# Two-layer transformer block with expert routing: five of six modulation products move from TensorE to folded row sums on VectorE, and three expert loads wait for stored rows

## The reference, cut to what matters

```
silu_c = jax.nn.silu(c)
silu_cc = jax.nn.silu(c_ctx)
for l in range(DEPTH):                       # DEPTH = 2
    mod = silu_c @ w_ada[l] + b_ada[l]
    sh1, sc1, gt1, sh2, sc2, gt2 = [m[:, None, :] for m in jnp.split(mod, 6, axis=-1)]
    modc = silu_cc @ w_ada[l] + b_ada[l]
    shc1, scc1, gtc1, shc2, scc2, gtc2 = jnp.split(modc, 6)
    h = modulate(rmsnorm(x, g_mix[l]), sh1, sc1)
    p = h @ w_in[l]
    x = x + gt1 * latent_mixer(p, ...)       # attention, windowed attention, short conv; gates; w_out
    h2 = modulate(rmsnorm(x, g_ffn[l]), sh2, sc2)
    x = x + gt2 * expert_choice_ffn(h2, ...) # router, top-k tokens of each of 16 experts, 3 matmuls
    # in layer 0 the same for the ctx tokens, with shc1 ... gtc2
```

## Time and profile before

| what | value |
|---|---|
| median of 3 runs | 3529.16 us (3526.13 to 3535.64) |
| the profiled execution's own time | 3529.06 us |
| its span | 3527.3 us |
| TensorE busy | 3276.5 us, 93% of the span |
| VectorE busy | 1242.0 us, 35% |
| ScalarE busy | 1004.1 us, 28% |
| mean granted TensorE clock | 0.979 of 2.4 GHz |
| DMA | 617.00 MB |

### The profile page before, as it was taken

How to read it: one execution, slowest core, us unless ns; L and a number is a source line. 1 busy time by engine, 2 the same in 40 slices (tenths; PEclk the granted TensorE clock), 3 DMA queues, 4 the chain that set the end, 5 groups by cost and what they waited for, 6 DMA issues and landing times.

```text
span 3527.3 us, 48003 instructions
## 1 busy us (share of the span) xinstructions
PE 3276.5 (93%) x21246; PEld 2201.5 (62%) x21250; DVE 1242.0 (35%) x1821; ACT 1004.1 (28%) x1571; POOL 221.3 (6%) x142
## 2 busy tenths in 40 slices
PE   6999999999699999989999996988879999989998
PEld 4787667888334343467768882332327766858887
DVE  3335642233401011145563333111126444353333
ACT  3623541122210001037343222000022354342223
POOL 0100000121000000001000220000002010020000
PEclk9999999999799999999999998999999999999999
DMA  7540014221899999743102329999983121323331
GB/s 216 149 144 25 1 49 120 66 61 60 323 399 398 390 351 395 299 65 83 39 1 72 96 90 370 421 421 421 421 321 86 34 59 37 96 60 96 101 96 66
DMA packets 385614, 617.00 MB, mean 175 GB/s; under 512 B 99234, under 2 KB 288896, under 8 KB 360704
## 3 DMA queue, kind: packets, MB, share of 16 engines
q1 hardware_dynamic: 378064, 596.50, 47.9%
q0 software_dynamic: 4384, 15.73, 1.3%
q10 hardware_dynamic: 2960, 1.71, 0.2%
HBM read 606.54 MB, written 7.34 MB: 174 GB/s over the span
## 4 chain that ended last, share of the span: by engine, by line
PE 81%; DMA 10%; DVE 4%; ACT 3%; issue 1%; ACTq 0%; POOL 0%; SPq 0%; DVEq 0%
PE ps L592 32%; PE ps L1844 6%; PE ps L2228 5%; PE ps L1083 4%; DMA ring<-in_w_e_up 4%; PE ps L1172 3%; PE ps L1847 3%; PE ps L644 3%; DMA ring<-in_w_e_down 3%; PE ps L1880 3%; PE ps L1133 3%; PE ps L1347 3%; PE ps L1839 2%; PE ps L613 2%; PE ps L1885 2%; PE ps L1876 2%
## 5 line engine op out<-in xcount | busy, mean ns | idle before, releaser
L592 PE MATMUL ps<-xh,wh 128*128 128x512 f32 x1912 | 635.2, 370 | 25.1 <-DVE xl L2074 14.8
L592 PE MATMUL ps<-xh,wl 128*128 128x512 f32 x1912 | 628.3, 367 | 0.0
L592 PE MATMUL ps<-xl,wh 128*128 128x512 f32 x1912 | 627.7, 366 | 0.0
L565 DVE TENSOR_TENSOR wl<-ring,wh 128x1024 fp32r<-128x1024 f32 (+1 forms) x259 | 333.0, 1286 | 443.1 <-ACT wh L556 441.5
L592 PEld LDWEIGHTS ps<-xh,wh 128*128 128x128 f32 x1912 | 329.3, 188 | 106.8 <-issue 25.9
L556 ACT ACTIVATE wh<-ring 128x1024 fp32r<-128x1024 f32 (+1 forms) x259 | 272.0, 1050 | 422.2 <-PE ps L592 162.7
L592 PEld LDWEIGHTS ps<-xh,wl 128*128 128x128 f32 x1912 | 328.8, 188 | 60.3
L592 PEld LDWEIGHTS ps<-xl,wh 128*128 128x128 f32 x1912 | 328.3, 188 | 58.1 <-issue 0.5
L1844 PE MATMUL ps<-ring,arena 128*32 128x512 f32 x1344 | 176.8, 598 | 0.9 <-ACT arena L1592 0.9
L1839 PE MATMUL ps<-ring,arena 128*64 128x512 f32 x704 | 162.7, 604 | 12.5 <-DMA ring<-in_w_e_up 8.0
L1094 DVE TENSOR_REDUCE sm<-ps 128x2 f32<-128x1536 f32 (+3 forms) x96 | 142.3, 1482 | 45.4 <-PE ps L1083 45.0
(11 more groups left out here) (277 smaller groups left out, 4444.4 us busy)
## 6 DMA issues: line engine op xcount, KB each, us to landing
ring<-in_w_e_gate SPq DMA_DIRECT2D x87, 1024.0 KB, 20.4
ring<-in_w_e_up SPq DMA_DIRECT2D x85, 1024.0 KB, 19.7
ring<-in_w_e_down SPq DMA_DIRECT2D x85, 1024.0 KB, 21.3
ring<-in_w_in SPq DMA_DIRECT2D x112, 512.0 KB, 4.0
ring<-in_w_ada SPq DMA_DIRECT2D x96, 512.0 KB, 4.9
arena<-in_w_e_up SPq DMA_DIRECT2D x43, 1024.0 KB, 17.4
arena<-in_w_e_down SPq DMA_DIRECT2D x43, 1024.0 KB, 20.7
arena<-in_w_e_gate SPq DMA_DIRECT2D x41, 1024.0 KB, 20.0
```

The lines of the kernel that those rows point to most:

```text
L565: e.tensor_tensor(in_heads(X, u, m.WL[:, o:o + many]), heads_of(X, u, halves.aps[s], many), in_heads(X, u, m.WH[:, o:o + many].bitcast(F32 ...
L592: i = e.matmul(ps[0:M, a:b], w[:, k, 0:M], h[:, k, a:b], start=k == 0 and p == 0, stop=k == 7 and p == 2)
```

## The change

1. Pairs 1 to 5 no longer go to TensorE. A new `dve_mod_part` takes a load of 256 rows x 512 columns of `w_ada` (two k of a quarter g of a pair; the same bytes as before) from the ring and, for each k, multiplies with the conditioning number of each partition and adds to `ACC` (128 x 512): `tensor_scalar` at k = 0, `scalar_tensor_tensor` (STT) for the other seven, for two vectors in pairs 1 to 3 and for one in pairs 4 and 5. When a quarter's eight k are in, `transpose` (32 x 32 blocks, all 128 x 512) and `tensor_reduce` (to 128 x 16) follow for each vector, one after the other, since both use `TR`.
2. At a pair's end TensorE folds the four row groups with four small matmuls (`pe_fold`), and VectorE adds the bias (`dve_fold`). `act_mod` and `pe_modt` stay for pair 0 only, and no bank is held through the later pairs.
3. The quarters' places: q0 and q1 of pair 1 in conv steps 0 to 7 (a load each); ten quarters in gate steps 0 to 19 of layer 0; eight in gate steps 0 to 15 of layer 1 (two loads each, at the end of VectorE's step). `pe_choice(0)` has no modulation left, and SP's list has no `w_ada` between the last "o" load and the experts' loads.
4. In layer 1, slots 11, 13 and 14 wait for `s_hs` 160, all rows stored, instead of the last transposed rows.

```diff
+        ACC = [tmp[:, 4352 + 512 * i:4864 + 512 * i] for i in (0, 1)]
+        MODS = [(pair, q) for pair in range(1, 6) for q in range(4)]
+        vectors = lambda g: (0, 1) if MODS[g][0] < 4 else (0,)
...
+        def mods_beside_conv(j):
+            return [(j // 4, j % 4)] if j < 8 else []
+        def mods_beside_gate(l, t):
+            i = t // 2
+            return [((2, 12)[l] + i, 2 * (t % 2) + c) for c in (0, 1)] if i < (10, 8)[l] else []
...
+        def dve_mod_part(e, X, g, c):
+            s, srcs, many, kind, what, arrived = X.pieces[X.plain["mods", g, c]]
+            e.wait_ge(*arrived)
+            for k in (2 * c, 2 * c + 1):
+                src = halves.aps[s][:, 512 * (k % 2):512 * (k % 2) + 512]
+                for w in vectors(g):
+                    if k == 0:
...
+                        e.tensor_scalar(ACC[w], src, csv[:, 0, w:w + 1], None, ALU.mult).then_inc(*d_md.up("mod", g, k, w))
+                        continue
+                    e.wait_ge(*d_md.at("mod", g, k - 1, w))
+                    e.scalar_tensor_tensor(out=ACC[w], in0=src, scalar=csv[:, k, w:w + 1], in1=ACC[w], op0=ALU.mult,
+                                           op1=ALU.add).then_inc(*d_md.up("mod", g, k, w))
+            if c < 3:
+                return
...
+            for w in vectors(g):
...
+                e.transpose(TR, ACC[w]).then_inc(*d_md.up("turn", g, w))
+                e.wait_ge(*d_md.at("turn", g, w))
+                e.tensor_reduce(RS[:, pair % 2, q, w], TR.rearrange("p (b i) -> p b i", i=32), AX, ALU.add).then_inc(*d_md.up("sum", g, w))
...
+            for g in range(4):
+                i = e.matmul(ps[32 * g:32 * g + 32, 0:16 * many].rearrange("p (q w k) -> p q w k", q=4, w=many), K("fold"), sums[:, g],
+                             start=True, stop=True)
...
@@ pe_proj
-                mods(n)
...
-                mods(10 + j)
@@ dve_proj, at the end of conv step j
-                mods(10 + j)
+                for g, part_ in mods_beside_conv(j) if l == 0 else ():
+                    dve_mod_part(e, X, g, part_)
@@ pe_merge
-                    if l == 0 and t < 8:
-                        pe_mod(e, 48 + 2 * t)
+                    for pair in folds_beside_gate(l, t):
+                        pe_fold(e, pair)
...
-                    if l == 0 and t < 8:
-                        pe_mod(e, 49 + 2 * t)
...
-                for m in range(64, 68):
-                    pe_mod(e, m)
@@ dve_merge, at the end of step t
                         weigh(br, d - 1)
                         dve_low(e, X, X.unit["b", br, d] + 1)
                         weigh(br, d)
+                    for g, part in mods_beside_gate(l, t):
+                        dve_mod_part(e, X, g, part)
@@ pe_choice
-            mods(*range(68, 80))
...
-            mods(*range(80, 88))
...
-            mods(*range(88, 96))
@@ sp_experts
                 elif l and s in (11, 13, 14):
-                    e.wait_ge(*p_rt.at("e1", "h2", 3))
+                    e.wait_ge(s_hs, 160)
```

More of the change, by code:

```diff
@@ new lines, in pe_modt, with dve_mod @@
+        def pe_modt(e):
+            ps, when = bank.take("modt", d_mod.at("mod", 0, 1))
+            for w in when:
+                e.wait_ge(*w)
+            e.wait_ge(*c_mod.at("mod"))
+            for c in range(4):
+                i = e.transpose(ps[:, 128 * c:128 * c + 128], MR0[:, 128 * c:128 * c + 128], ident)
+            i.then_inc(*p_modt.up("mod", 0))
+        def dve_mod(e):
+            e.wait_ge(*p_modt.at("mod", 0))
+            pv = bank.of["modt"][:, 0:512].rearrange("p (n h g w) -> p n g h w", n=2, h=2, g=4)
+            for nb in (0, 1):
+                o = modv[:, 0, 8 * nb:8 * nb + 8, :].rearrange("p (g h) w -> p g h w", h=2)
+                b = PT[:, 32 + 8 * nb:40 + 8 * nb].rearrange("p (g h) -> p g h", h=2)
+                e.tensor_tensor(o, pv[:, nb, :, :, 0:2], b.unsqueeze(3).broadcast_to([128, 4, 2, 2]),
+                                ALU.add).then_inc(*d_mod.up("mod", 0, nb))
+            dve_gain(e, 0)
@@ L678, in pe_modt, with pe_fold @@
+        def pe_fold(e, pair):
             ps, when = bank.take(("modt", pair), d_mod.at("mod", pair, 1))
@@ L680, in pe_modt @@
                 e.wait_ge(*w)
-            e.wait_ge(*c_mod.at("mod", pair))
-            for c in range(4):
-                i = e.transpose(ps[:, 128 * c:128 * c + 128], MR(pair)[:, 128 * c:128 * c + 128], ident)
+            g = MODS.index((pair, 3))
+            many = len(vectors(g))
+            e.wait_ge(*d_md.at("sum", g, many - 1))
+            sums = RS[:, pair % 2, :, 0:many].rearrange("p q w (k g) -> p g q w k", g=4)
+            for g in range(4):
+                i = e.matmul(ps[32 * g:32 * g + 32, 0:16 * many].rearrange("p (q w k) -> p q w k", q=4, w=many), K("fold"), sums[:, g],
+                             start=True, stop=True)
@@ L684, in pe_modt, with dve_fold @@
             i.then_inc(*p_modt.up("mod", pair))
-        def dve_mod(e, pair):
+        def dve_fold(e, pair):
             l, n2 = pair // 3, pair % 3
+            many = len(vectors(MODS.index((pair, 3))))
             e.wait_ge(*p_modt.at("mod", pair))
[L689 to L695, removed]
-            if n2 != 1:
[L697 to L701, removed]
@@ L1443, in dve_merge @@
                     dve_low(e, X, X.unit["g", br, d] + 1)
-                    if l == 0 and t == 8:
-                        dve_mod(e, 3)
+                    for pair in folds_beside_gate(l, t - 1):
+                        dve_fold(e, pair)
                     if d % 2:
```

120 lines of the change are left out of this document (52 added, 68 removed).

## The result

The changed kernel takes 3558.03 us (median of 4 runs, 3556.60 to 3558.81), the one before 3527.64; the ratio is 1.0085, with a 95% interval of 1.0073 to 1.0097. That is 30 us slower by the medians and 27.4 by the spans of the two profiles (3554.7 and 3527.3). Forecast were 3568 us and a loss of 39. One odd execution in each of two sets, 8301 us in experiment 1 and 3821 us in the runs of the kernel before that experiments 1, 2, 3 and 6 were timed beside, is in the medians and not in the ratios.

A forecast was written before the change was run, and what follows sets the result against it. It took TensorE to bound roped, conv and merge stages, and waits on tiles, loads, stores and gathers the choices. Stalls 61 plus clock 34 minus gains 56 gave +39 on 3529.06, 3568 us; range 3524 to 3590, main case 3545 to 3585.

The forecast's parts named there:

- Gains: Whole kernel: time saved in roped and conv, layer 0's merge and both layers' choices, 56 us.
- Roped and conv: Roped and conv stages: sixteen pairs of modulation tiles leave TensorE at 1.2 us a pair, 19 us gained.
- Merge of layer 0: Layer 0's merge: tiles, the pair's copy and what it held up go, 14.5 and 2.4 us, together 17.
- Choice of layer 0: Layer 0's choice: no tiles or their transposes, and expert loads issued well before the gather, 17.5 us gained.
- the 3.8 for the gather: Layer 0's choice: SP issues expert loads some 40 us before the gather, saving 3.8 us (bounds 0 and 3.9).
- Choice of layer 1: Layer 1's choice: three loads behind the stores let the gather start earlier, 2.7 us gained (bounds 0 and 4.2).
- VectorE's chain: Layer 0's merge: branch product's end through weighing, eight products and quarter's end to `wl`, 10.6 us against 8.4 cover.
- the rival of dear transposes: VectorE's quarter ends: transposes at twice the shuffle's time, 22 us more, 3590 us; chance 0.11.
- Stalls: TensorE waits for late `wl`: 39 us in layer 0, 19 in layer 1, 2 in conv, 1 for folds; 61.
- The clock: Behind TensorE's stalls: half clock loses 1.7 us after seven short, 2.5 after nine longer ones; 34 us, bounds nothing and 40.
- Stalls without the clock: Rival for the whole kernel: stalls come but cost no clock, +5, 3534 us; chance 0.17.
- VectorE is in time: Rival in the merges: VectorE's chain stays under 8.4 and 5.45 us, no stall, -55, 3474 us; chance 0.12.

The follow-up runs named there:

- experiment 1: Changed kernel with all VectorE products and quarter's ends written behind the next step's first `wl` in conv and merges, loads reordered to match: 3475.13 us, ratio 0.9849.
- experiment 2: Changed kernel with only the quarter's ends (transposes and sums) moved behind the next `wl`, the products left in place: 3501.66 us, ratio 0.9921.
- experiment 3: Changed kernel with GpSimd's addition of an odd step waiting until VectorE has ended that step's quarter: 3536.89 us, ratio 1.0026.
- experiment 6: Changed kernel with part 4 taken back, layer 1's three loads again waiting for the last transposed rows, beside the stores: 3561.15 us, ratio 1.0093.
- experiment 7: experiment 1 with SP's first expert load of layer 0 waiting for the indices, so loads go beside the gather: 3482.77 us, ratio 0.9870.
- experiment 5: experiment 1 with most products cut to 16 of 512 columns and filler transposes before the gate unit's `wl`, two kernels: 3545.68 and 3536.18 us.
- the kernel of many lengths: First kernel of experiment 5, with different numbers of filler transposes so that TensorE's stalls get many lengths: 3545.68 us, one run.

## Why the prediction was right, and where it was off

The time, 3558, is 10 us below the forecast and well inside its own range of 3545 to 3585. The steps one by one:

- **Gains, 56 forecast, 53.2 measured.** Experiment 1 shows the first two bare. Roped and conv: 238.1 to 218.9 us, 19.2 (forecast 19). Merge of layer 0 up to "o": 320.0 to 306.1, 13.8 (17). Its first ten steps, which had the tiles, gave 15.9 of the forecast 2.4 + 14.5; the others, which had none, take 2.0 longer than before, 25.27 us instead of 25.12 for two steps and 25.71 where a fold lies in them. The "o" units take 66.8 us in experiment 1 and 68.1 in the kernels before and after, at a granted clock of 1.00 in all three; the cause of this is open, and the changed kernel doesn't have that 1.3. Choice of layer 0: 17.8 (17.5). Of this the 3.8 for the gather is shown by experiment 7. Choice of layer 1: 2.4 in the pair of profiles, 2.8 over all of them (2.7).
- **VectorE's chain, 10.6 forecast, 10.3 measured.** Eight products 5.4 and 5.38, transpose 0.73 and 0.71, sum 0.7 and 0.69. The transpose, which no row showed, cost what the shuffle of the earlier trace rows costs; the rival of dear transposes falls.
- **Stalls, 61 forecast, 55.7 measured** (35.9, 17.6 and 2.2). Each of layer 0 was 0.2 to 0.6 shorter (1.99 for 2.2, 3.57 for 3.9, 5.45 for 5.7, 7.06 for 7.4). The folds that lie inside a stall cost nothing: the stall is 1.75 there instead of 1.99, and 3.33 instead of 3.57. The one of layer 0 outside costs some 0.4. The stalls' cause is shown by experiments 1 and 2, GpSimd's share by experiment 3.
- **The clock, 34 forecast, 27.7 measured.** This is the term that was mis-sized. By the units of experiment 1 (8.48 and 5.45 us) those behind a stall are 13.5 us longer in layer 0, 12 in layer 1 and 0.6 in conv; the "o" units of layer 1, 45.4 us instead of 43.8, make the other 1.6. About 3 of the 27.7 are the 0.1 to 0.2 that stand behind every stall. The prediction let every stall of about 2.3 us lose 1.7, and every longer one 2.5. Of the seven short ones four of those in the merges lost near 1.8 and two 0.1; the seven long ones of layer 0 lost 1.5 to 1.8 and not 2.5, the two of layer 1 3.0 and 2.6. Experiment 5 shows why the first can't be told from a length.
- **The rivals.** "Stalls without the clock" (3534) would have been the result without those 27.7, by which it is 3530; no run has these stalls and a full clock. "VectorE is in time" is experiment 1: 3475 against the 3474 that the prediction gave this case. Its verdict that it would take 2.2 us less per quarter was right for this order of the program, and missed that the order was free.

The sum closes: 55.7 + 27.7 - 53.2 = 30.2, and with the +2.5 before the first "v" and the -5.4 of the four untouched stretches 27.3, against 27.4 in the profiles. That the forecast came within 10 us is in part luck: its losses were 11.6 us too large and its gains 2.8, so that 3 of the 12 cancelled. The mechanism, stalls behind a quarter's end that outweigh the gains, is as forecast.

## What to carry to other kernels

VectorE's busy share (35%) said that there was room for the products, and there was; but an engine that works in its written order needs the room at the place. Before adding work to it, write down from one handed-over buffer to the next what stands in between and how long the consumer is covered, and put the new work right behind the hand-over with the longest cover, not at the end of the step that it belongs to. In experiment 5 a stall of 1.7 to 3.2 us on TensorE cost its length and in about half of the cases another 1.6 to 1.9 us, nearly all of it for the clock. And when a load is moved out of one transfer's way, look at what it meets next: a gather of 4.4 us took 8.5 with seven loads beside it, and behind three loads it ended some 11 us after the first of them; but loads that the experts wait for cost more when late than the gather gains.

## What the runs showed of the hardware

- A `tensor_scalar` of 128x512, float32, with one input in SBUF, was held by GpSimd's addition as well: two took 2.46 us instead of 0.88 (experiment 3, where the addition's row stands beside it). Twelve transposes of 128x512 beside such an addition took 8.65 us, 0.72 each, and were not held (experiment 5, the kernel of many lengths):

```profile
609.57 8.65 DVE L725 STREAM_TRANSPOSE tmp<-tmp 128x512 f32<-128x512 f32 x12
```
```profile
609.73 1.86 POOL L1529 TENSOR_TENSOR arena<-arena,tmp 128x768 f32<-128x768 f32 x1 [1.40 <-DVE tmp L1484]
```

  The same section of the Trainium skill lists `tensor_scalar` among the operations that can take GpSimd's port in a fast mode; the rows agree.
- Nine stalls of 2.7 to 2.9 us left the granted clock of the next 3.6 us at 1.00 five times and at 0.54 to 0.59 four times, in turn (experiment 5).
- The gather took 8.36 us behind seven 1 MB loads (the kernel before, the last load issued 0.8 us ahead of it) and 8.47 among seven (experiment 7, three ahead of it and four within 2.1 us behind its start), and 4.2 to 4.7 us in twelve cases in which SP had issued no load within the 15 us before it. With three such loads, the first issued 3.2 to 6.5 us ahead, it took 7.9 to 4.7 us, and ended 11.0 to 11.3 us behind that first one in all eight cases.
